# One hybrid decoder layer: the opening, the low-rank gate products and the merged tiles are rearranged

## The reference

```python
z = rmsnorm(x, g_attn) @ w_in          # q, k, v, r of GLA | ga1 (16) | q, k, v of FoX | ff (8) | gate_a, gate_b
log_a = log_sigmoid(ga1 @ w_gla_a2 + b_gla_a) / 16      # (16 x 512): the "gate's second matrix", 4 heads x 128
lf = log_sigmoid(ff + b_fox_f)
o_gla = gla_chunked(q, k, v, log_a); o_fox = forgetting_attention(q, k, v, lf)
merged = sigmoid(gate_a) * (o_gla @ w_pa) + sigmoid(gate_b) * (o_fox @ w_pb)
x = x + merged @ w_o
x = x + (silu(h @ w_gate) * (h @ w_up)) @ w_down        # h = rmsnorm(x, g_ffn), D_FF = 5632
y = rmsnorm(x, g_final)
```

## Time and profile before

| | |
|---|---|
| time, median of 3 runs (lowest, highest) | 1846.05 us (1845.99, 1846.32) |
| the profiled execution: its time, its span | 1846.93 us, 1845.2 us |
| PE busy | 1826.8 us, 99% |
| DVE, ACT, POOL busy | 968.5, 686.2, 26.5 us |
| granted TensorE clock, mean | 0.996 of full |
| DMA | 295 MB, mean 160 GB/s |

### The profile page before, as it was taken

One profiled execution on the slowest core, in us unless ns is written; L12 is line 12 of the kernel. 1 busy time (PEld: TensorE's weight loads), 2 busy tenths in 40 slices (PEclk: granted clock), 3 DMA queues, 4 the chain that ended last, 5 costly groups with the idle time before them and its releaser, 6 DMA issues.

```text
span 1845.2 us, 31153 instructions
## 1 busy us (share of the span) xinstructions
PE 1826.8 (99%) x12940; PEld 1797.2 (97%) x12940; DVE 968.5 (52%) x1374; ACT 686.2 (37%) x947; POOL 26.5 (1%) x65
## 2 busy tenths in 40 slices
PE   8999999999999999999999999999999999999997
PEld 8999999999999999999999999999999999999996
DVE  7755464455447544665544444444444444454455
ACT  6433333333333343344433333333333333333353
POOL 4000000000000000000000000000000000000000
PEclk9999999999999999999999999999999999999998
DMA  7564565437455644554454355443554445544453
GB/s 251 153 202 149 169 194 183 166 131 231 148 168 191 185 139 148 180 174 149 137 161 153 122 155 168 156 149 125 149 173 151 147 136 148 174 143 155 128 149 112
DMA packets 129343, 295.26 MB, mean 160 GB/s; under 512 B 15770, under 2 KB 59298, under 8 KB 129202
## 3 DMA queue, kind: packets, MB, share of 16 engines
q1 hardware_dynamic: 121666, 284.54, 48.6%
q10 hardware_dynamic: 7504, 8.72, 1.3%
q0 software_dynamic: 32, 0.01, 0.0%
HBM read 283.25 MB, written 9.97 MB: 159 GB/s over the span
## 4 chain that ended last, share of the span: by engine, by line
PE 99%; DVE 0%; DMA 0%; ACT 0%; DVEq 0%; SPq 0%; issue 0%
PE banks L1097 31%; PE banks L1099 31%; PE banks L1098 31%; PE banks L1110 3%; PE banks L1107 1%; DMA weights_raw<-in_w_project 0%; PE banks L1333 0%; PE banks L1335 0%; PE banks L1334 0%; PE banks L1196 0%; DVE gates L1084 0%; PE banks L1126 0%; DVEq L113 0%; DVE weights_low L668 0%; ACT weights_high L456 0%
## 5 line engine op out<-in xcount | busy, mean ns | idle before, releaser
L668 DVE TENSOR_TENSOR weights_low<-weights_raw,weights_high 128x1024 fp32r<-128x1024 f32 (+2 forms) x530 | 607.6, 1147 | 564.2 <-ACT weights_high L456 560.6
L456 ACT ACTIVATE weights_high<-weights_raw 128x1024 fp32r<-128x1024 f32 (+2 forms) x530 | 524.6, 991 | 608.7 <-PE banks L1099 599.5
L1097 PE MATMUL banks<-a_high,weights_high 128*128 128x320 f32 x2224 | 703.8, 316 | 0.0
L1099 PE MATMUL banks<-a_high,weights_low 128*128 128x320 f32 x2224 | 687.2, 309 | 0.0
L1098 PE MATMUL banks<-a_low,weights_high 128*128 128x320 f32 x2224 | 687.0, 309 | 0.0
L1097 PE MATMUL banks<-b_high,weights_high 128*128 128x320 f32 x1664 | 514.9, 309 | 0.1
L1098 PE MATMUL banks<-b_low,weights_high 128*128 128x320 f32 x1664 | 514.2, 309 | 0.0
L1099 PE MATMUL banks<-b_high,weights_low 128*128 128x320 f32 x1664 | 514.2, 309 | 0.0
L1097 PEld LDWEIGHTS banks<-a_high,weights_high 128*128 128x128 f32 x2224 | 417.7, 188 | 8.9 <-issue 6.6
L1098 PEld LDWEIGHTS banks<-a_low,weights_high 128*128 128x128 f32 x2224 | 418.1, 188 | 0.3
L1099 PEld LDWEIGHTS banks<-a_high,weights_low 128*128 128x128 f32 x2224 | 417.5, 188 | 0.0
(11 more groups left out here) (219 smaller groups left out, 673.9 us busy)
## 6 DMA issues: line engine op xcount, KB each, us to landing
weights_raw<-in_w_gate_up SPq DMA_DIRECT2D x176, 512.0 KB, 3.4
weights_raw<-in_w_project SPq DMA_DIRECT2D x160, 512.0 KB, 3.5
weights_raw<-in_w_down_a SPq DMA_DIRECT2D x64, 384.0 KB, 3.2
weights_raw<-in_w_down_b SPq DMA_DIRECT2D x64, 320.0 KB, 2.9
weights_raw<-in_w_merge SPq DMA_DIRECT2D x32, 512.0 KB, 3.3
weights_raw<-in_w_out SPq DMA_DIRECT2D x32, 512.0 KB, 3.4
area<-in_cache_kT SPq DMA_DIRECT2D x128, 64.0 KB, 2.5
area<-in_cache_v SPq DMA_DIRECT2D x128, 64.0 KB, 2.8
```

The source lines that it names most:

```text
L456: act.activation(high[:, u % SLOTS, 0:n], raw[:, u % SLOTS, 0:n], ACT.Copy).then_inc(on["high_ready"], 1)
L668: dve.tensor_tensor(low[:, u % SLOTS, 0:n], raw[:, u % SLOTS, 0:n], high[:, u % SLOTS, 0:n].bitcast(F32), ALU.subtract).then_inc(on["low_r ...
L1097: pe.matmul(bank(b, 0, T), w_high, x_high[:, k, :], start=first and n == 0, stop=False, skip_group_check=True)
L1099: done = pe.matmul(bank(b, 0, T), w_low, x_high[:, k, :], start=False, stop=last and n == tiles - 1, skip_group_check=True)
```

## The change

```diff
+UNIT_BEHIND_X = {1: 1, 3: 2, 5: 3}
...
-        w_a2 = spare[32:32 + RANK, 1216:1728]
-        ga1 = spare[32:32 + RANK, 1728:2048]
+        w_a2 = spare[0:80, 1216:1728]
+        ga1 = spare[0:80, 1728:2048]
+        a2_parts = b_high[0:80, KT - 4:KT - 2, :].rearrange("p a b -> p (a b)")[:, 0:GH * DK]
+        ga1_parts = b_low[0:80, KT - 4, :]
+        idle = b_low[:, 0:2, :].rearrange("p a b -> p (a b)")[:, 0:512]
...
         @block.sync
...
-            sp.dma_start(pages[:, :], page_table...).then_inc(on["pages_landed"], 16)
-            load(0, w_narrow[0])
+            first_units = (w_narrow[0], w_project[0], w_narrow[1], w_project[1])
+            load(0, first_units[0])
             for c in range(8):
                 sp.dma_start(x_raw[:, 2 * c:2 * c + 2, :], xT[:, 2 * c:2 * c + 2, :]).then_inc(on[f"x_landed_{c}"], 16)
-                if c == 0:
-                    load(1, w_project[0])
-                if c == 3:
-                    load(2, w_narrow[1])
-                if c == 5:
-                    load(3, w_project[1])
+                if c in UNIT_BEHIND_X:
+                    u = UNIT_BEHIND_X[c]
+                    load(u, first_units[u])
+            load(SLOTS, w_project[SLOTS - U_PROJECT])
             sp.wait_ge(on["pages_landed"], 16)
...
-                if n == NB:
-                    load(SLOTS, w_project[SLOTS - U_PROJECT])
+                if n == NB // 2:
+                    load(SLOTS + 1, w_project[SLOTS + 1 - U_PROJECT])
...
         @block.gpsimd
...
+            pool.memset(idle.bitcast(F32), 1.0).then_inc(on["idle_ready"], 1)
             pool.memset(ones[:, :], 1.0).then_inc(on["ones_ready"], 1)
...
+            pool.memset(w_a2, 0.0).then_inc(on["a2_zeroed"], 1)
...
         @block.scalar
...
                 if s < 2:
-                    for c in ((2, 3, 4), (5, 6, 7))[s]:
+                    for c in range(4 * s, 4 * s + 4):
                         square_x(c)
                 if s == 3:
-                    act.wait_ge(on["x_low_ready"], KT)
-                    act.wait_ge(on["x_squared"], KT // 2)
-                    act.dma_start(w_a2, w_gla_a2[:, :]).then_inc(on["a2_landed"], 16)
+                    act.wait_ge(on["a2_zeroed"], 1)
+                    for r in range(3):
+                        act.dma_start(w_a2[32 * r:32 * r + RANK, :], w_gla_a2[:, :]).then_inc(on["a2_landed"], 16)
+                if s == 8:
+                    act.wait_ge(on["ga1_ready"], 1)
+                    act.wait_ge(on["a2_landed"], 48)
+                    act.activation(ga1_parts, ga1, ACT.Copy).then_inc(on["ga1_high_ready"], 1)
+                    act.activation(a2_parts, w_a2, ACT.Copy).then_inc(on["a2_high_ready"], 1)
...
             act.dma_start(gains[:, :], gains_in[:, :]).then_inc(on["gains_landed"], 16)
+            act.dma_start(pages[:, :], page_table...).then_inc(on["pages_landed"], 16)
...
-                if c in (0, 3, 4):
-                    prepare(1 + (0, 3, 4).index(c))
-            square_x(0)
-            square_x(1)
+                if c in UNIT_BEHIND_X:
+                    prepare(UNIT_BEHIND_X[c])
...
-                if s >= KT + 1:
-                    merged_high(s - KT - 1)
+                if s >= KT + 2:
+                    merged_high(s - KT - 2)
             for s in range(2 * KT):
                 prepare(U_OUT + s + LEAD)
                 if s == 0:
+                    merged_high(KT - 2)
                     merged_high(KT - 1)
...
         @block.vector
...
-                    dve.tensor_tensor(ga1, psum[32:32 + RANK, 6, 0:T], rstd_x[32:32 + RANK, :], ALU.mult
+                    dve.tensor_tensor(ga1, bank(6, 0, T, 80), rstd_x[0:80, :], ALU.mult
...
-                    link(dve.tensor_tensor(z_row, bank(6, 0, T, FH), rstd_x[0:FH, :], ALU.mult))
+                    link(dve.tensor_tensor(z_row, psum[96:96 + FH, 6, 0:T], rstd_x[96:96 + FH, :], ALU.mult))
...
+                if s == 10:
+                    dve.wait_ge(on["a2_high_ready"], 1)
+                    dve.wait_ge(on["ga1_high_ready"], 1)
+                    dve.tensor_tensor(ga1_parts[32:32 + RANK, :], ga1[32:32 + RANK, :], ga1_parts[32:32 + RANK, :].bitcast(F32), ALU.subtract
+                                      ).then_inc(on["a2_parts_ready"], 1)
+                    dve.tensor_tensor(a2_parts[64:64 + RANK, :], w_a2[64:64 + RANK, :], a2_parts[64:64 + RANK, :].bitcast(F32), ALU.subtract
+                                      ).then_inc(on["a2_parts_ready"], 1)
...
         @block.tensor
...
-                if (s, n) in ((5, 4), (22, 4), (23, 4), (24, 4)):
+                if (s, n) in ((5, 6), (22, 4), (23, 4), (24, 4)):
                     h = (5, 22, 23, 24).index(s)
                     if h == 0:
-                        pe.wait_ge(on["a2_landed"], 16)
+                        pe.wait_ge(on["a2_landed"], 48)
                         pe.wait_ge(on["ga1_ready"], 1)
+                        pe.matmul(bank(2, 0, T), w_a2[0:RANK, 0:DK], ga1[0:RANK, :], start=True, stop=True
+                                  ).then_inc(on["a2_multiplied"], 1)
+                    else:
+                        if h == 1:
+                            pe.wait_ge(on["bias_ready"], 1)
+                            pe.wait_ge(on["a2_parts_ready"], 2)
...
-                    pe.matmul(bank(3 if h else 2, 0, T), w_a2[:, h * DK:(h + 1) * DK], ga1, start=True, stop=True
+                        pe.matmul(bank(3, 0, T), a2_parts[:, h * DK:(h + 1) * DK], ga1_parts, start=True, stop=True
...
-            pe.wait_ge(on["ones_ready"], 1)
-            for n in range(13):
-                add(bank(7, 0, P), ones[:, :], ones[:, :], start=True, stop=True)
-            for c in range(KT // 2):
-                for u, b in ((2 * (c // 4), 6), (2 * (c // 4) + 1, J_PROJECT % 2)):
+            pe.wait_ge(on["idle_ready"], 1)
+            def warm(times, columns):
+                for n in range(times):
+                    add(bank(7, 0, columns), idle[:, 0:P], idle[:, 0:columns], start=True, stop=True)
+            warm(13, 512)
+            warm(5, 256)
+            steps = [(c, narrow) for c in range(KT // 2) for narrow in (True, False)]
+            steps[1], steps[2] = steps[2], steps[1]
+            for c, narrow in steps:
+                u, b = (2 * (c // 4), 6) if narrow else (2 * (c // 4) + 1, J_PROJECT % 2)
...
+                if narrow and c < 2:
+                    warm((1, 4)[c], 512)
...
 def _lay_out(inputs):
...
-    narrow[:, 0:FH] = w_in[:, FF:FF + FH]
-    narrow[:, 32:32 + RANK] = w_in[:, GA1:GA1 + RANK]
+    narrow[:, 96:96 + FH] = w_in[:, FF:FF + FH]
+    for r in range(3):
+        narrow[:, 32 * r:32 * r + RANK] = w_in[:, GA1:GA1 + RANK]
```

More of the change, by code:

```diff
@@ L291, in _ @@
                     u = U_PROJECT + TURN_UNITS * i + s
-                    if u > SLOTS:
+                    if u > SLOTS + 1:
                         load(u, w_project[u - U_PROJECT])
@@ L583, in _ @@
             act.dma_start(gains[:, :], gains_in[:, :]).then_inc(on["gains_landed"], 16)
+            act.dma_start(pages[:, :], page_table.rearrange("b g -> (b g)").rearrange("(o n) -> o n", o=1)
+                          ).then_inc(on["pages_landed"], 16)
             prepare(0)
@@ L1019, in _ @@
                     gate_b_read(s - KT - 1)
-                if s > KT + 1:
-                    merged_low(s - KT - 2)
+                if s > KT + 2:
+                    merged_low(s - KT - 3)
             for s in range(2 * KT):
@@ L1026, in _ @@
                     gate_b_read(KT - 1)
+                    merged_low(KT - 3)
                     merged_low(KT - 2)
@@ L1317, in project_between @@
                     fox(i, j, s - at, n)
-            pe.wait_ge(on["ones_ready"], 1)
-            for n in range(13):
-                add(bank(7, 0, P), ones[:, :], ones[:, :], start=True, stop=True)
-            for c in range(KT // 2):
-                for u, b in ((2 * (c // 4), 6), (2 * (c // 4) + 1, J_PROJECT % 2)):
-                    pe.wait_ge(on["low_ready"], u + 1)
-                    for k in (2 * c, 2 * c + 1):
-                        pe.wait_ge(on["x_low_ready"], k + 1)
-                        n = k % UNIT
-                        w_high = high[:, u, n * P:(n + 1) * P]
-                        w_low = low[:, u, n * P:(n + 1) * P]
-                        pe.matmul(bank(b, 0, T), w_high, a_high[:, k, :], start=k == 0, stop=False, skip_group_check=True)
-                        pe.matmul(bank(b, 0, T), w_high, a_low[:, k, :], start=False, stop=False, skip_group_check=True)
-                        done = pe.matmul(bank(b, 0, T), w_low, a_high[:, k, :], start=False, stop=k == KT - 1, skip_group_check=True)
-                        if n == UNIT - 1:
-                            done.then_inc(on["units_multiplied"], 1)
+            pe.wait_ge(on["idle_ready"], 1)
@@ new lines, in warm @@
+            def warm(times, columns):
[7 more added lines that the diff above has]
```

(14 more changed lines are left out.)

12 lines of the change are left out of this document (4 added, 8 removed).

## The result

| | before | changed |
|---|---|---|
| time, median of 7 runs each | 1846.76 us (1845.99 to 1847.88) | 1840.62 us (1840.15 to 1841.12) |
| ratio to before, 95% interval | | 0.9966 (0.9956 to 0.9976) |
| profiled execution, its span | 1845.2 us | 1839.0 us |

What follows compares the result with a forecast made beforehand. TensorE's stream was taken to bound the kernel, with VectorE's chain limiting the opening: 1.15 (opening) + 2.33 (stacked products) + 1.5 (merged tiles) = 5.0 us off 1846.05, giving 1841.0; range 1839.8 to 1842.6.

Steps and rivals of the forecast that it cites:

- What bounds: Whole kernel: TensorE (PE) is busy 99% of the span, so only shortening its stream or its few gaps can show.
- VectorE's chain: Opening, squares' sum to the read of K: comes 1.15 us earlier and sets the opening's gain, from 0.35 to 2.0.
- Three stacked products, 2.33: Three later heads' gate products: f32r instead of f32 saves 0.78 us each, 2.33 in all; 2.07 if weight loads are late.
- Merged tiles, 1.5: Merge: a step's delay opens the ScalarE-VectorE ring of 3.81 us against PE's 3.52, removing 1.5 us of waits (1.3 to 1.5).
- The clock: PE's opening: clock stays full after 1.6 us idle, so 14 products no longer run at half clock; 1.65 us saved.
- wrong if under 10.9: Sign for the opening: first wide product starts at 11.5 us; wrong if under 10.9 or over 12.
- its first rival: Opening: the clock falls at 11 us all the same, 1.65 us come back, giving 1841.9; chance 0.12.
- PE waits for VectorE at the sum and at the GLA block: End of opening: PE waits 0.35 us at the summed squares and has no slack at the GLA turn.
- at about 32.1: Sign for the opening: PE's product of summed squares comes at about 32.1 us, with a wait on VectorE before it.
- so all that follows comes 0.41 earlier: Opening loads: SP issues unit 0 in the page table's place, at 0.81 instead of 1.22, moving all that follows 0.41 us.
- The upper bound of the opening, 2.0: Opening: PE's own gain of 2.0 us, from 1.65 (clock) and 0.88 (six products earlier) less 0.54.
- rival 2: Opening: VectorE's chain is no bound and PE keeps its whole 2.0 us, giving 1840.2; chance 0.08.

Runs made afterwards that it cites:

- e5: Changed kernel with the three later heads' gate products in plain f32 on 16 rows again; median 1842.62 us.
- e4: Changed kernel with the merged tiles' high and low parts one step earlier, as before the change; median 1842.03 us.
- e1: Changed kernel without its five idle products between the first pairs of the opening; median 1840.59 us.
- e9: Changed kernel with PE's old order in the opening and without the five idle products between; loads, preparations and first idle group as changed; median 1840.74 us.
- e3: Changed kernel with the old opening loads and preparations on SP, ScalarE and VectorE, page table first; PE's order and idle products as changed; median 1842.72 us.
- e8: Changed kernel with the product of the summed squares and turn 0's GLA block each one tile later; median 1840.10 us.
- e6: Changed kernel with the page table's DMA first in SP's queue again, instead of second in ScalarE's; median 1841.51 us.
- e7: Changed kernel with unit 1 issued and prepared behind pair 0 of x instead of pair 1; median 1841.13 us.
- e11: Changed kernel with unit 1 behind pair 0, PE's old order without idle products between, and later squares' product, first gate product and GLA block; median 1840.12 us.

## Why the prediction came out as it did

- **What bounds.** Right: PE's stream, and three places in it. Every gain on PE reached the end except where VectorE's chain stood.
- **Three stacked products, 2.33.** Right, 2.21: 0.77, 0.68 and 0.76. The second is followed at once by a transposition, a plain f32 product itself, and the first f32r product behind f32 takes 0.10 more than its like (113.92 to 114.17, 0.25 for 0.147): there that price stayed. The measured rows decided it. By the four passes that the Trainium skill ("FP8 and Floating Point Precision", TensorE Precision Notes) states, the estimate was 1.32 for the three, and the traces do not agree: 2.21, and 2.20 in e5.
- **Merged tiles, 1.5.** Right, by its mechanism and size: 1.54, undone by e4 to 1.53.
- **The clock.** The forecast (full, 1.65 us saved on PE) was right, the working not: it had PE idle for 1.6 us behind the five idle products, and there was no idle stretch, since the first wide product came at 10.50 and not at 11.5. By the prediction's own sign (wrong if under 10.9) this step is wrong. The traces of e1 and e9 show that the idle products between are not what keeps the clock. Against its first rival the prediction says that times within 0.33 us speak against a clock that falls in some executions only. That rested on three executions: with more, the kernel before goes from 1845.77 to 1847.95 us, at mean granted clocks from 0.998 to 0.995, and e3 has one execution apart from nine. So a fall that comes and goes is likely but not shown, and the changed kernel has no such gap.
- **PE waits for VectorE at the sum and at the GLA block.** Right in kind: 0.17 for 0.35 forecast, and no slack at the block, where PE waits 0.25. e8 shows that a tile each removes them. The sign for the first, "at about 32.1", does not fit the prediction's own sum: 33.28 less 1.65 is 31.6; 30.57 was measured.
- **The step that failed: "so all that follows comes 0.41 earlier".** Taking the page table from the head of SP's queue was worth 1.2 us in the median and moved unit 1 by 1.4 to 2.0 in the traced execution, not 0.41 (e6). The other half of the sum, 0.95 for pair 1 ahead of unit 1, fits: 8.59 before, 9.50 with pair 1 ahead and the table still first (+0.91; +1.19 from e3's 8.31). Unit 1 came at 8.13 instead of 9.13, unit 3 without a wait instead of at 14.85, ScalarE's squares at 17.85, 0.9 us ahead of the forecast (18.7), and the chain is 2.45 earlier instead of 1.15. The upper bound of the opening, 2.0, was PE's own gain built on the same 0.41; 2.87 measured. By the medians this step accounts for 0.8 (1.2 less 0.4) of the 1.1 us by which the gain exceeds the forecast.

Of the forecast gains, rival 2's (PE's gain comes through whole, 5.85 us) came closest to 6.1, but not by its mechanism: VectorE's chain still bounds, it only moved nearly as far as PE. What stays open is why the first transfer in the queue costs so much; shown is only that less is moved between 4 and 6 us.

## What to carry to other kernels

Where an opening waits for its first loads, measure what stands at the head of the DMA queue by taking it away; its own issue time is no price for it. Reorder loads, preparations and PE's products together, and look at which side is then last: here two waits on VectorE's chain, 0.42 us together, were left, and one tile's delay on PE at each place covers them. Compare the traced execution's time with the median before reading a loss from it: e3's was 1.5 us away. A step whose wait crosses two engines and comes back can be opened by one step of delay, and that gain can be computed from the two periods (3.81 and 3.52 us) and the number of rounds that wait (five and a partial one here).

## What the runs showed of the hardware that was not expected

- A transfer of 64 bytes at the head of the queue: 277 to 330 GB/s between 4 and 6 us, against 345 to 406 without it; unit 1 behind it 1.4 to 2.0 us later in the one trace that differs in this alone, the kernel 1.2 later in the median. The gains' start in the other queue moves with it (1.84 against 2.61 us).
- The granted clock after idleness: full after 1.79 us idle behind six products (e9), half after 2.28 (e3) and 2.43 (before). These are one execution each, and in e3 the nine others' times say that it most likely did not fall there.
- The moment at which the first idle products were given the full clock lay anywhere from 4.2 to 7.5 us in the fourteen profiled executions. That is what the Trainium skill ("TensorE: Matmul & The Clock Gate", Part 1) says of the start, that the count of cold products is run-variable; the traces agree. In e7, the one at 7.5, the 18 idle products were themselves what the first real one came behind (7.88 instead of 7.4 to 7.6; in e11 it was 8.00, behind a late unit 0). The fall at 11 us came in both traced executions that idled over 2.2 us and in none of the twelve others.
- Unit 1 was taken up anywhere from 7.47 to 8.13 us in the eight executions with the changed kernel's opening loads, and in those that also had its order on PE the GLA block came anywhere from 49.75 to 50.41: single executions can't tell steps apart that move it by less.
